# Two sigmoid-gate projections moved into the last head's scan, and the later ones two tiles ahead, in the second mixer of a diffusion trunk

## The reference

```python
proj = u @ w_in
q, zf, zb, i, g, pv, ga, gb = jnp.split(proj, IN_SPLITS, axis=-1)
o, s_f, s_b = hgrn2_bidir(q, i, zf, zb, lb_f, lb_b, s0_f, s0_b)   # gated linear scan, 4 heads
on = o * lax.rsqrt(jnp.mean(o * o, axis=-1, keepdims=True) + EPS)
a = on * hg_norm_w * jax.nn.silu(g)                                # 512 wide
p = pool_mixer(pv, pool_w, pool_scale, on_grid)                    # box means, 512 wide
merged = jax.nn.sigmoid(ga) * (a @ w_a) + jax.nn.sigmoid(gb) * (p @ w_b)
return merged @ w_out, s_f, s_b
```

## Time and profile before

| | us |
|---|---|
| three executions: median (lowest to highest) | 1967.54 (1967.37 to 1968.43) |
| the profiled execution | 1972.28 |
| its span, from the first to the last instruction | 1970.6 |
| busy in the span: PE | 1940.4 (98%) |
| DVE | 1252.2 (64%) |
| ACT | 787.9 (40%) |

### The profile page before, as it was taken

How to read it: one execution, slowest core, us unless ns; L and a number is a source line. 1 busy time by engine, 2 the same in 40 slices (tenths; PEclk the granted TensorE clock), 3 DMA queues, 4 the chain that set the end, 5 groups by cost and what they waited for, 6 DMA issues and landing times.

```text
span 1970.6 us, 28334 instructions
## 1 busy us (share of the span) xinstructions
PE 1940.4 (98%) x9754; PEld 1636.9 (83%) x9754; DVE 1252.2 (64%) x2020; ACT 787.9 (40%) x1084; POOL 74.3 (4%) x145
## 2 busy tenths in 40 slices
PE   8999999999999999999999999999999999999998
PEld 3888888888888888888888888888888888899997
DVE  2657566677666466658566675765857778576555
ACT  2431322345564323541322354222224576455444
POOL 0001000000000000001000000000000000000000
PEclk8999999999999999999999999999999999999999
DMA  7345444533213243345444434544544333555654
GB/s 312 97 139 204 140 163 161 164 106 123 70 65 102 77 160 119 113 141 185 156 149 172 145 122 139 181 160 138 183 153 144 98 106 97 174 173 180 184 191 149
DMA packets 78120, 287.39 MB, mean 146 GB/s; under 512 B 8728, under 2 KB 8992, under 8 KB 77280
## 3 DMA queue, kind: packets, MB, share of 16 engines
q1 hardware_dynamic: 57760, 211.32, 32.7%
q0 software_dynamic: 19712, 74.40, 11.6%
q10 hardware_dynamic: 576, 0.70, 0.1%
HBM read 285.34 MB, written 1.05 MB: 145 GB/s over the span
## 4 chain that ended last, share of the span: by engine, by line
PE 94%; DMA 2%; DVE 2%; issue 1%; ACT 1%; SPq 0%; ACTq 0%; DVEq 0%
PE bank L366 26%; PE bank L367 26%; PE bank L368 26%; DMA raw<-weights 2%; PE bank L582 2%; PE bank L775 2%; PE bank L642 1%; PE bank L636 1%; PE bank L637 1%; PE bank L500 1%; PE bank L502 1%; PE bank L503 1%; PE bank L468 1%; ACT w_hi L797 1%; PE bank L719 1%
## 5 line engine op out<-in xcount | busy, mean ns | idle before, releaser
L366 PE MATMUL bank<-u_hi,w_hi 128*128 128x512 f32 (+1 forms) x1824 | 663.8, 364 | 0.3 <-DVE w_lo L1109 0.3
L368 PE MATMUL bank<-u_hi,w_lo 128*128 128x512 f32 (+1 forms) x1824 | 654.7, 359 | 0.0
L367 PE MATMUL bank<-u_lo,w_hi 128*128 128x512 f32 (+1 forms) x1824 | 654.6, 359 | 0.0
L1109 DVE TENSOR_TENSOR w_lo<-raw,w_hi 128x1024 fp32r<-128x1024 f32 x382 | 466.6, 1222 | 249.8 <-ACT w_hi L797 220.7
L797 ACT ACTIVATE w_hi<-raw 128x1024 fp32r<-128x1024 f32 x382 | 402.7, 1055 | 436.1 <-DMA raw<-weights 435.7
L366 PEld LDWEIGHTS bank<-u_hi,w_hi 128*128 128x128 f32 x1824 | 344.6, 189 | 51.1 <-issue 0.7
L368 PEld LDWEIGHTS bank<-u_hi,w_lo 128*128 128x128 f32 x1824 | 344.3, 189 | 51.3
L367 PEld LDWEIGHTS bank<-u_lo,w_hi 128*128 128x128 f32 x1824 | 344.7, 189 | 50.2 <-issue 0.7
L1120 DVE SCALAR_TENSOR_TENSOR junk<-ada_raw,silu_c 128x1024 bf16<-128x1024 f32 x256 | 298.1, 1220 | 0.0
L366 PE MATMUL bank<-hid_hi,w_hi 128*128 128x512 f32 (+1 forms) x656 | 249.0, 380 | 0.0
L367 PE MATMUL bank<-hid_lo,w_hi 128*128 128x512 f32 (+1 forms) x656 | 248.4, 379 | 0.0
(11 more groups left out here) (188 smaller groups left out, 1660.5 us busy)
## 6 DMA issues: line engine op xcount, KB each, us to landing
raw<-weights SPq DMA_DIRECT2D x382, 512.0 KB, 3.5
ada_raw<-adaw POOLq DMA_DIRECT2D x128, 512.0 KB, 4.3
start_w<-weights SPq DMA_DIRECT2D x8, 1024.0 KB, 12.2
box<-box POOLq DMA_DIRECT2D x4, 1024.0 KB, 8.1
h<-resid SPq DMA_DIRECT2D x1, 2048.0 KB, 19.3
silu_c<-c POOLq DMA_DIRECT2D x1, 1024.0 KB, 5.2
poolw<-poolw POOLq DMA_DIRECT2D x2, 256.0 KB, 10.4
gate_rows<-gate_dram POOLq DMA_DIRECT2D x1, 512.0 KB, 3.9
```

The costliest lines, as they stand in the source:

```text
L366: pe.matmul(ps, w_hi[:, slot, k, :], hi(k), start=first, stop=False)
L367: pe.matmul(ps, w_hi[:, slot, k, :], lo(k), start=False, stop=False)
L368: mm = pe.matmul(ps, w_lo[:, slot, k, :], hi(k), start=False, stop=last)
L1109: dve.tensor_tensor(view(w_lo, (j % RING) * UNIT, [1, UNIT]), raw[:, j % RING, :], view(w_hi, (j % RING) * UNIT, [1, UNIT]).bitcast(F32), ...
```

## The change

In the second layer two gate units of `gb` (0 and 1) stand in the last head, ahead of its pieces 4 and 8, in banks 0 and 1. Their splits on ACT and DVE stand there too. The last head has therefore eight units instead of six, and the numbers of the later ones move (`unit_at`). After the scan the units called gate 0 and 1 before are now gates 2 and 3. In the merge, branch d of the first four tiles is followed by gate d+4, and branches 4 to 7 follow each other (`branch_unit` gives their places). The gates' sigmoids are written to the unused half of `sig_a` instead of `sig_b`. The loops of the merge are written out instead of being hardware loops. The first layer keeps its order. The number of units, matmuls and splits is the same.

```diff
+def early_gates(layer):
+    return 2 if layer == NLAYER - 1 else 0
+def early_gate(layer, head, piece):
+    if early_gates(layer) and head == NH - 1 and piece in (4, 8):
+        return piece // 4 - 1
+    return None
+def unit_at(layer, head, j):
+    return j + (j // 2 if early_gates(layer) and head == NH - 1 else 0)
+def branch_unit(layer, d):
+    return 2 + d + min(d, ND - 2 - early_gates(layer))
```

On PE, in the last head's pieces:

```diff
+                        early = early_gate(layer, head, piece)
+                        if early is not None:
+                            pe.wait_ge(s_sga, layer * ND + 2 * head + early + 1)
+                            u = unit_at(layer, head, j) - 1
+                            gate_b(bank[early], (unit + u) % RING, unit + u + 1)
+                        u = unit_at(layer, head, j)
```

On PE, in the merge (`ng` is the number of early gates of the layer):

```diff
+                if ng:
+                    for d in range(ND):
+                        at = branch_unit(layer, d)
+                        branches(d // 2, d % 2, unit % RING + at, at)
+                        if d < ND - 2 - ng:
+                            pe.wait_ge(s_sgb, layer * ND + ng + d + 1)
+                            gate_b(bank[4 * (d % 2)], (unit + at + 1) % RING, unit + at + 2)
```

On ACT, in the pieces:

```diff
+                        early = early_gate(layer, head, piece)
+                        if early is not None:
+                            split_unit(base + u - 1 + AHEAD)
                         if piece % 2:
-                            split_next(base + j - (base + j) % 4, None, (base + j) % 4 + AHEAD)
+                            split_unit(base + u + AHEAD)
                         if piece < NLEVEL:
                             mix_directions(n, piece + 1, nt)
+                        early = early_gate(layer, head, piece - 1)
+                        if early is not None:
+                            gate_b(bank[early], early, base + u)
```

On ACT, in the merge:

```diff
+                if ng:
+                    for d in range(ND):
+                        at = branch_unit(layer, d)
+                        split_unit(base + at + AHEAD)
+                        if d < ND - 2 - ng:
+                            act.wait_ge(s_mg, layer * ND + d + 3)
+                            gate_b(bank[4 * (d % 2)], d + ng + 2, base + at + 2)
+                        merged_hi(d)
+                        if d < ND - 2 - ng:
+                            split_unit(base + at + 1 + AHEAD)
```

On DVE, in the pieces:

```diff
+                        if early_gate(layer, head, piece) is not None:
+                            split_unit(base + u - 1 + AHEAD)
```

On DVE, in the merge:

```diff
+                if ng:
+                    for d in range(ND):
+                        at = branch_unit(layer, d)
+                        split_unit(base + at + AHEAD)
+                        if d:
+                            merged_lo(d - 1)
+                        merge_branches(d // 2, d % 2, None, at)
+                        if d < ND - 2 - ng:
+                            split_unit(base + at + 1 + AHEAD)
+                    merged_lo(ND - 1)
```

On the host, the order of the units:

```diff
+            units += [wga[6:8], wgb[0:1], wide(wpv)[0:2], wgb[1:2], wide(wpv)[2:4]]
...
+        units.append(wgb[ng:ng + 2])
+        units.append(np.stack([branch[:ND - 2 - ng], wgb[2 + ng:]], 1).reshape(2 * (ND - 2 - ng), P, UNIT))
+        units.append(branch[ND - 2 - ng:])
```

More of the change, by code:

```diff
@@ L662, in mixer, with gate_b @@
                 unit += 4
+                def gate_b(ps, slot, unit_wait):
+                    half(ps[:, 0:nt], slot, 0, ND, hi(nt), lo(nt), unit_wait, done=True)
                 for head in range(NH):
@@ L690, in mixer @@
                                     pe.wait_ge(s_sga, layer * ND + 2 * head - 1 + j)
-                            half(bank[b][:, 0:m], (unit + j) % RING, k0, k0 + 4, hi(m), lo(m),
-                                 unit + j + 1 if not second else None, done=bool(second),
+                            half(bank[b][:, 0:m], (unit + u) % RING, k0, k0 + 4, hi(m), lo(m),
+                                 unit + u + 1 if not second else None, done=bool(second),
                                  start=not second, stop=bool(second))
@@ L696, in mixer @@
                                 pe.wait_ge(s_sga, layer * ND + ND - 1)
-                            natural(PV_BANK, unit + j, j - 2, ntile, (second, second + 1),
+                            natural(PV_BANK, unit + u, j - 2, ntile, (second, second + 1),
                                     bank_wait=(1, s_sga, layer * ND + ND))
@@ L708, in mixer @@
                     unit += 6
-                def gate_b(ps, slot, unit_wait):
-                    half(ps[:, 0:nt], slot, 0, ND, hi(nt), lo(nt), unit_wait, done=True)
-                gate_b(bank[GATE_BANK[0]], 0, unit + 1)
+                ng = early_gates(layer)
+                unit += ng
+                gate_b(bank[GATE_BANK[0]], unit % RING, unit + 1)
                 pe.wait_ge(s_box, 48 * (layer + 1))
@@ L721, in mixer @@
                     mm.then_inc(s_dmm, 1)
-                gate_b(bank[GATE_BANK[1]], 1, unit + 2)
+                gate_b(bank[GATE_BANK[1]], (unit + 1) % RING, unit + 2)
                 head_spread(layer, NH - 1)
@@ L731, in mixer, with branches @@
                               start=True, stop=True).then_inc(s_pmm, 1)
-                def branches(i, b, at):
+                def branches(i, b, at, here=None):
+                    wait = i * 4 + (unit + at + 1) if here is None else unit + here + 1
                     pe.wait_ge(s_mg, i * 2 + (layer * ND + b + 1))
                     half(bank[4 * b + 1][:, 0:nt], at % RING, 0, 4, lambda k: a_hi[:, k, 0:nt],
-                         lambda k: a_lo[:, k, 0:nt], i * 4 + (unit + at + 1))
+                         lambda k: a_lo[:, k, 0:nt], wait)
                     if b == 0:
@@ L742, in branches @@
                          lambda k: p_lo[:, k - 4, 0:nt], None, done=True)
-                with pe.Fori(0, ND // 2 - 1) as i:
-                    for b in range(2):
-                        branches(i, b, 2 + 2 * b)
-                        pe.wait_ge(s_sgb, i * 2 + (layer * ND + b + 1))
-                        gate_b(bank[4 * b], 3 - 2 * b, i * 4 + (unit + 2 * b + 4))
-                for b in range(2):
-                    branches(ND // 2 - 1, b, 2 + b)
-                unit += 2 * ND
+                if ng:
[5 more added lines that the diff above has]
+                            gate_b(bank[4 * (d % 2)], (unit + at + 1) % RING, unit + at + 2)
+                else:
+                    with pe.Fori(0, ND // 2 - 1) as i:
+                        for b in range(2):
+                            branches(i, b, 2 + 2 * b)
+                            pe.wait_ge(s_sgb, i * 2 + (layer * ND + b + 1))
+                            gate_b(bank[4 * b], 3 - 2 * b, i * 4 + (unit + 2 * b + 4))
+                    for b in range(2):
+                        branches(ND // 2 - 1, b, 2 + b)
+                unit += 2 * ND - ng
                 res = res_count(layer, 0) + 3 * ND
@@ L961, in mixer, with split_unit, gate_b @@
                 base += 4
+                ng = early_gates(layer)
+                def split_unit(u):
+                    split_next(u // RING * RING, None, u % RING)
+                def gate_b(ps, d, unit_used):
+                    act.wait_ge(s_used, unit_used)
+                    gate = sig_a[:, d, TOK:ALL] if ng else sig_b[:, d, 0:nt]
+                    act.activation(gate, ps[:, 0:nt], ACT.Sigmoid).then_inc(s_sgb, 1)
                 for head in range(NH):
@@ L1457, in merged_lo, with merge_branches @@
                         ALU.subtract).then_inc(s_ulo, 1)
-                def merge_branches(i, b, at):
-                    dve.wait_ge(s_used, i * 4 + (base + at + 1))
+                def merge_branches(i, b, at, here=None):
+                    gate = sig_a[:, 2 * i + b, TOK:ALL] if ng else sig_b[:, b, 0:nt]
+                    dve.wait_ge(s_used, i * 4 + (base + at + 1) if here is None else base + here + 1)
                     sa = sig_a[:, bass.ds(i * 2 + b, 1), 0:nt].rearrange("p a n -> p (a n)")
@@ L1464, in merge_branches @@
                     dve.wait_ge(s_sgb, i * 2 + (layer * ND + b + 1))
[L1465 removed]
+                    dve.tensor_tensor(mix_t[:, b, 1, 0:nt], gate, bank[4 * b + 2][:, 0:nt],
                                       ALU.mult).then_inc(s_mt, 1)
```

79 lines of the change are left out of this document (42 added, 37 removed).

## The result

| | us, median (lowest to highest) | executions |
|---|---|---|
| changed kernel | 1976.51 (1974.76 to 1980.73) | 8 |
| kernel before, beside it | 1971.22 (1967.37 to 1972.23) | 8 |

The ratio is 1.0036 (95% interval 1.0025 to 1.0046): the change makes the kernel 7.1 us slower (4.9 to 9.1). Forecast were 1972.9 us, in a range of 1969.6 to 1975.4, and 5.4 us slower. The sign was right, the time lies 3.6 us off and outside the range. The ratio weighs all the executions: the means, 1977.29 and 1970.22, are 7.1 us apart too, while the medians are only 5.3 apart. One execution of the kernel before, beside e0 to e3, took 2425.52 us at a granted clock of 0.751 and is left out of every ratio.

A forecast was written before the change was run, and what follows sets the result against it. PE was taken to bound the kernel (94% of the last chain), with ACT and DVE bounding the scan. Box means +5.79, two units fewer -5.76 and merge idle +5.33 gave +5.36 on 1967.54: 1972.9 us, range 1969.6 to 1975.4.

The forecast's parts named there:

- steps 5 and 7 later by gate 0: Last head's scan: a DVE split ahead of `prepare_step` 5 delays step 5 and the scan behind it by 1.14 us.
- load in front of `AX`, issue to split: Last head, piece 9: the load ACT splits before copying `AX` takes 7.59 us from issue to split.
- wait before the head's output: Last head's output step: PE waits 3.2 us for `AX`, bounds 0 and 3.6.
- box means later: After the last head: the 1.36 us wait is covered and the box means start 5.79 us later.
- last merges apart: Last merges: sums follow each other every 4.13 us a tile, against 2.88 of PE work.
- first branch to tile 7's products: From first branch into the output projection: two units fewer, -5.76 us, and more PE idle time, +5.33.
- from there to the norm's totals: Behind PE's products of tile 7, up to the next norm's totals: no change, 0 us.
- The copy to `AX` gets a load in front of it: Last head, piece 9: ACT's split waits for a late load, delaying `AX`; output step 7.30 us later, box means 5.79.
- The merge: After gate 7: merge, `m_hi`, both splits, `m_lo`, next merge form a ring; PE idles 6.90 us, before 1.57: +5.33.
- Rivals 1 and 3: First (20%): load before `AX` takes its DMA share at once, 1970.2 us; second (4%): also no merge ring, 1963.7 us.
- Rival 2: Last merges: PE's branches set the pace, tiles turned around in under 2.88 us; not slower, 1966.4 us; 8%.
- rival 4: Before the pooling weights: delayed `AX` pushes further loads and splits past their slack of about 1 us; +8, 1975.5 us; 8%.

The follow-up runs named there:

- e0: The changed kernel run again unedited, as control for three edits on the same chip: 1980.33 us, ratio 1.0055 to the kernel before.
- e3: Changed kernel with matmuls on data nobody reads put into TensorE's waits before the last head's output and in the merge and output: ratio 1.0035 to the kernel before.
- e1: Changed kernel with ScalarE copying `AX` before it splits the unit behind gate 1, last head of the second layer: ratio 1.0022 to the kernel before.
- e2: Changed kernel with the last four merges done before the splits that stood ahead of them: ratio 1.0010 to the kernel before.
- e8: Kernel before, with ScalarE copying `AX` six extra times ahead of the real copy in the second layer's last head: ratio 1.0012 to the kernel before.
- e5: Changed kernel with the box tables' transfer held back in the second layer until the last head's state step is scored: 1977.75 us, ratio 1.0035 to the kernel before.
- e9: Kernel before, with three extra `AX` copies by ScalarE ahead of the real one in the second layer's last head: ratio 1.0001 to the kernel before.
- e6: Kernel before, with the second layer's last `m_lo` put ahead of the split before it on VectorE: ratio 1.0002 to the kernel before.
- e4: Changed kernel with both the `AX` copy and the last four merges put before their splits: 1964.91 us, ratio 0.9975 to the kernel before.
- e7: As e4, but with only gate 0 multiplied early, ahead of piece 4: 1969.79 us, ratio 0.9991 to the kernel before.

## Why the prediction was wrong

The steps of the sum, against the traces:

| step | predicted | measured |
|---|---|---|
| steps 5 and 7 later by gate 0 | 1.14 | 1.16 (1676.41 - 1664.23 against 1680.05 - 1669.03) |
| load in front of `AX`, issue to split | 7.59 | 7.68 |
| wait before the head's output | 3.2 | 3.30 |
| head's output later | 7.30 | 7.31 |
| box means later | 5.79 | 7.50 |
| last merges apart | 4.13 | 4.11 to 4.12 |
| first branch to tile 7's products | -0.43 | -0.58 (1750.55 - 1706.55 against 44.58) |
| from there to the norm's totals | 0 | +2.14 (23.58 against 21.44) |

The waits that the change makes and their causes were right. So were their sizes, within 0.15 us: the forecast's 1.9 and 1.2 us before branches 6 and 7 and 3.5 in the first output unit are shown as 1.62, 0.99 and 3.08, and each shown wait is 0.16 short, the overlap that the prediction names. The failed step is one that the sum made without saying so: **it let TensorE's work behind a wait take as long as before**. "The copy to `AX` gets a load in front of it" let the `pv` half and the gate unit after the head's output run at full rate (+1.71 on the box means), and "The merge" ended its count at the last wait, as if nothing were lost behind it (+2.14). The trace's 8.98 exceeds 5.36 by 3.62, and these two are 1.71 + 2.14 = 3.85 of it, with -0.23 of small differences. e3 shows that this part is the clock, since it goes away when the waits are filled; e1, e2 and e8 each give its size at one wait (1.87, 2.6 and 1.76).

The base is a second failed step, and in the number it weighs as much. 1967.54 was the median of three executions, though the profiled one took 1972.28, and beside the changed kernel the median was 1971.22: 3.7 us higher, where the time missed by 3.6. With that base the same sum would have been 1976.6, almost the measured 1976.51. That would have been luck, since the sum lacks the half clock: the kernel before runs near 1967.5 or 1971.5 (last section), so its median moves with how many executions fall on either side. The medians (5.3 us apart) and the interval of 4.9 to 9.1 us do not refute the 5.4; e0's ratio (8.1 to 13.6 us slower) and the traces, counted from step 3, do.

Rivals 1 and 3 (the load takes its share at once) fell by the 7.68 us, and e5 shows that the tables' transfer is the cause. The rule of the Trainium skill's page "DMA: Bandwidth & Descriptors" (section "Queues, rings and completion order"), turns packet by packet between queues, doesn't describe what this load got: 7.68 us from issue to split, against 3.58 in e5. Rival 2 (the ring doesn't close) fell by the merges' distance, and rival 4 had about its slower time but not its reason: between the head's output and branch 6 TensorE waited for nothing.

## What to carry to other kernels

A wait of TensorE has two prices, its length and what the clock takes behind it: here waits of 3.17 us and more, or 5.69 in four pieces, cost 1.8 to 3.2 us again. Single waits of 1.29 (e9) and 1.84 us (e6) had no half clock behind them, but one of 1.79 (e5) had, so a short wait is not safe by its length. Work moved into TensorE's idle time paid here only once the orders on the other engines moved with it: a split stood in front of a copy and another in front of a merge, with no data between them, and turning both around made a loss of 7.1 us a gain of 4.9.

## What the runs showed of the hardware

The kernel before has executions of 1966.4 to 1968.7 us and of 1969.9 to 1974.9 us, and none of the 76 lies between. The traces show where: at the first norm. TensorE waits 3.45 or 3.46 us for `u_hi` in all twelve traces, and the granted clock is low around that. The 4 us rows of the kernel before, and then of e6, whose code is the same there:

```profile
36.00:40.00 4.00, 4.00 (x27) 3.12 (x25) 1.87 (x3) 1.48 (x3) 0.00 (x0) 0.90 0.02 4
40.00:44.00 4.00, 4.00 (x20) 4.00 (x20) 1.09 (x4) 3.05 (x5) 2.27 (x4) 0.50 0.30 125
44.00:48.00 4.00, 3.42 (x11) 2.50 (x11) 2.41 (x6) 0.00 (x0) 0.00 (x0) 0.50 0.99 409
48.00:52.00 4.00, 1.11 (x5) 1.15 (x6) 4.00 (x8) 1.71 (x4) 0.00 (x0) 0.50 0.26 108
52.00:56.00 4.00, 4.00 (x15) 3.52 (x14) 4.00 (x11) 2.08 (x5) 0.00 (x0) 0.50 0.00 0
```

```profile
36.00:40.00 4.00, 4.00 (x34) 3.68 (x33) 1.77 (x4) 2.10 (x4) 0.00 (x0) 1.00 0.02 4
40.00:44.00 4.00, 4.00 (x22) 3.18 (x21) 2.33 (x8) 2.43 (x3) 2.26 (x4) 0.70 0.48 197
44.00:48.00 4.00, 0.54 (x3) 0.47 (x3) 4.00 (x8) 1.09 (x3) 0.00 (x0) 0.50 1.04 419
48.00:52.00 4.00, 4.00 (x17) 3.67 (x17) 4.00 (x12) 2.44 (x6) 0.00 (x0) 0.52 0.07 25
52.00:56.00 4.00, 4.00 (x19) 3.29 (x18) 4.00 (x11) 2.25 (x6) 0.00 (x0) 1.00 0.00 0
```

In the first the clock is below 1.00 from before 40 us and at 0.50 until about 56, in the second from after 40 until about 52, the work behind the wait starts at 50.88 and 47.56, and step 3 of the last scan comes at 1669.03 and 1665.63. The twelve traces fall into these kinds: before, e3, e4, e5, e7 and e9 have the long spell and step 3 at 1668.3 to 1670.3; the changed kernel, e1, e2, e6 and e8 have the short one and step 3 at 1664.2 to 1665.7; e0, at 1666.67, is between. In the changed kernel that work starts at 47.82, 3.06 us earlier than in the kernel before, which is most of the 4.80 us by which its step 3 was early. It differs between executions of the same code, and is a reason to count from a mark near the change. What decides which kind an execution gets was not tried.
